# Weight sums of a fast block product: two of four formed by accumulating transfers from GpSimd's queue

## The reference

```python
def swiglu(h, w_gate_up, w_down):
    gu = h @ w_gate_up                     # (512, 1024) @ (1024, 2 * 2816)
    g, u = gu[..., :D_FF], gu[..., D_FF:]
    return (jax.nn.silu(g) * u) @ w_down
```

## Time and profile before

| | |
|---|---|
| median of 3 runs | 1385.08 us (1385.01 to 1385.16) |
| span of the profiled execution, first to last instruction | 1383.4 us |
| own time of the profiled execution beside its span | not listed apart; the runs' median is 1.7 us above the span |
| busy: PE, DVE, ACT, POOL | 1374.1, 961.5, 663.8, 114.9 us |
| granted clock of TensorE, mean of the span | 0.998 of full speed |
| DMA moved | 147.22 MB, mean 106 GB/s |
| transfers issued by GpSimd | none |

### The profile page before, as it was taken

The page is one execution under the profiler, slowest core; times in us unless marked ns, Lnnn a source line. Parts: engine busy times, 40 slices in busy tenths (PEclk is TensorE's granted clock), DMA queues, the critical chain, the costliest instruction groups (busy, mean ns, idle before and its releaser), DMA issues.

```text
span 1383.4 us, 21582 instructions
## 1 busy us (share of the span) xinstructions
PE 1374.1 (99%) x8404; PEld 1225.5 (89%) x8404; DVE 961.5 (70%) x1335; ACT 663.8 (48%) x984; POOL 114.9 (8%) x89
## 2 busy tenths in 40 slices
PE   9999999999999999999999999999999999999997
PEld 8988888889999998998887788988888999998897
DVE  6656556469878877774578755765549888888674
ACT  6633534355455553352756634543454545545341
POOL 0012200110000000110211211100020000000011
PEclk9999999999999999999999999999999999999999
DMA  9721320222323233325321212542132223233321
GB/s 345 268 91 61 107 92 31 91 92 77 122 92 122 93 107 107 120 95 167 97 87 46 82 41 77 185 150 77 46 107 79 105 98 116 93 122 98 116 92 62
DMA packets 42285, 147.22 MB, mean 106 GB/s; under 512 B 5072, under 2 KB 5584, under 8 KB 42192
## 3 DMA queue, kind: packets, MB, share of 16 engines
q1 hardware_dynamic: 38592, 136.79, 28.8%
q10 hardware_dynamic: 3600, 9.12, 1.9%
HBM read 143.80 MB, written 2.10 MB: 105 GB/s over the span
## 4 chain that ended last, share of the span: by engine, by line
PE 96%; DVE 2%; issue 1%; ACT 1%; DMA 0%; POOLq 0%; POOL 0%; ACTq 0%; DVEq 0%
PE acc L2173 17%; PE acc L2175 17%; PE acc L2174 17%; PE acc L2521 8%; PE acc L2522 7%; PE acc L2523 7%; PE acc L2221 3%; PE acc L2223 3%; PE acc L2222 3%; PE aux L2572 2%; PE aux L2571 2%; PE aux L2570 2%; PE aux L2523 1%; PE aux L2522 1%; PE aux L2521 1%
## 5 line engine op out<-in xcount | busy, mean ns | idle before, releaser
L1304 DVE TENSOR_TENSOR w_lo<-raw,w_hi 128x1024 fp32r<-128x1024 f32 x165 | 205.6, 1251 | 123.6 <-ACT w_hi L663 123.2
L663 ACT ACTIVATE w_hi<-raw 128x1024 fp32r<-128x1024 f32 x165 | 173.2, 1052 | 98.6 <-PE acc L2175 55.2
L1229 POOL TENSOR_TENSOR sqsum<-sqsum,tmp 128x512 f32<-128x512 f32 x40 | 60.0, 1501 | 960.3 <-ACT tmp L950 637.0
L2173 PE MATMUL acc<-u_hi,w_hi 128*128 128x512 f32 x352 | 138.7, 394 | 0.0
L2175 PE MATMUL acc<-u_hi,w_lo 128*128 128x512 f32 x352 | 137.2, 390 | 0.0
L2174 PE MATMUL acc<-u_lo,w_hi 128*128 128x512 f32 x352 | 137.1, 389 | 0.0
L2521 PE MATMUL acc<-b_hi,s_hi 128*128 128x256 f32 x432 | 122.4, 283 | 0.0
L2522 PE MATMUL acc<-b_lo,w_hi 128*128 128x256 f32 x432 | 122.3, 283 | 0.0
L2522 PE MATMUL acc<-b_lo,s_hi 128*128 128x256 f32 x432 | 122.2, 283 | 0.0
L2523 PE MATMUL acc<-b_hi,w_lo 128*128 128x256 f32 x432 | 122.2, 283 | 0.0
L2523 PE MATMUL acc<-b_hi,s_lo 128*128 128x256 f32 x432 | 122.2, 283 | 0.0
(11 more groups left out here) (311 smaller groups left out, 3611.0 us busy)
## 6 DMA issues: line engine op xcount, KB each, us to landing
raw<-in_weights SPq DMA_DIRECT2D x253, 512.0 KB, 3.4
hT<-in_x_t ACTq DMA_DIRECT2D x4, 512.0 KB, 8.2
x_tok<-in_x ACTq DMA_DIRECT2D x4, 512.0 KB, 5.1
raw<-in_weights SPq DMA_DIRECT2D x5, 256.0 KB, 6.1
mem_tok<-in_mem ACTq DMA_DIRECT2D x2, 512.0 KB, 5.8
out_h<-out_f SPq DMA_DIRECT2D x2, 512.0 KB, 2.6
memT<-in_mem_t SPq DMA_DIRECT2D x3, 256.0 KB, 6.3
cs_d<-in_cs_d ACTq DMA_DIRECT2D x1, 512.0 KB, 4.3
```

The costliest lines, as they stand in the source:

```text
L663: act.activation(w_hi[:, s, :], raw[:, s, :], ACT.Copy).then_inc(hi_ready, 1)
L1229: pool.tensor_tensor(sqsum[:, :], sqsum[:, :], tmp[:, j % 2, :], ALU.add).then_inc(sq_added, 1)
L1304: dve.tensor_tensor(w_lo[:, s, :], raw[:, s, :], w_hi[:, s, :].bitcast(F32), ALU.subtract)\
L2173: pe.matmul(out, w_h, x_h, start=first, stop=False)
```

## The change

For the pairs q = 2 to 17 of each layer, the first sum (y0 + y1) and the sum that replaces y1 in the ring (x0 + y1) are made by transfers. `weight_sums` on GpSimd's queue, called for q = 2 to 17 behind the layer's last norm: once the plain part's last product is there (`prod_ready`) and, for q of 4 and above, once the low parts of the sums of pair q - 2 are there (`slo_ready`), it issues a transfer of y0 from HBM into the buffer `pre_sum(q)`, which is `sqsum` for even q and `rstd_row` for odd q. Once y has landed in its slot (`raw_in`), it issues a transfer that adds x0 from HBM onto the second half of y in the ring (`third_in`). Once the first transfer has landed (`pre_in`), it issues one that adds y1 from HBM onto `pre_sum(q)`. Each is 128x512 values, 256 KB. ScalarE's `pair_hi` waits for `third_in` in place of `s3_ready`. VectorE's `first_sums` waits for `pre_in` and makes one add, out of `pre_sum(q)` and x0. The high and the low parts of the sums are made by two instructions each, of 512 columns (from `pre_sum`) and of 1024 (from `s_f`). Pairs 0 and 1 of a layer stay as they are, and so do TensorE's instructions and SyncE's loads.

```diff
--- before.py
+++ after.py
@@ -350,6 +350,8 @@
         bhi_ready = sem("bhi_ready")
         blo_ready = sem("blo_ready")
         s3_ready = sem("s3_ready")
+        pre_in = [sem(f"pre_in{e}") for e in range(2)]
+        third_in = [sem(f"third_in{e}") for e in range(2)]
         s_ready = sem("s_ready")
         shi_ready = sem("shi_ready")
         slo_ready = sem("slo_ready")
@@ -478,6 +480,14 @@
 
             n = pair_unit(layer, q) % RING
             return ring[:, n:n + 2, :]
+
+        def pre_sum(q):
+
+            return (sqsum, rstd_row)[q % 2]
+
+        def nth(layer, q):
+
+            return (PAIRS // 2 - 1) * layer + q // 2
 
         def region_a(q):
             return accs[2 * (q % 2)][:, 0:S // 2]
@@ -865,7 +875,10 @@
 
                     n = pair_unit(layer, q)
                     act.wait_ge(raw_in[n % RING], 16 * (n // RING + 1))
-                    act.wait_ge(s3_ready, PAIRS * layer + q + 1)
+                    if q < 2:
+                        act.wait_ge(s3_ready, 2 * layer + q + 1)
+                    else:
+                        act.wait_ge(third_in[q % 2], 16 * nth(layer, q))
                     slot_free(act, n - RING)
                     slot_free(act, n + 1 - RING)
                     act.activation(pair_cols(w_hi, layer, q), pair_cols(raw, layer, q), ACT.Copy).then_inc(hi_ready, 2)
@@ -873,7 +886,10 @@
                 def sum_hi(q):
 
                     act.wait_ge(s_ready, PAIRS * layer + q + 1)
-                    act.activation(s_hi[q % 2][:, :, :], s_f[q % 2][:, :, :], ACT.Copy).then_inc(shi_ready, 1)
+                    if q >= 2:
+                        act.activation(s_hi[q % 2][:, 0, :], pre_sum(q)[:, :], ACT.Copy)
+                    b = slice(1 if q >= 2 else 0, 3)
+                    act.activation(s_hi[q % 2][:, b, :], s_f[q % 2][:, b, :], ACT.Copy).then_inc(shi_ready, 1)
 
                 def copy_product(q, m):
 
@@ -1228,6 +1244,20 @@
                         pool.wait_ge(sq_added, n - 1)
                     pool.tensor_tensor(sqsum[:, :], sqsum[:, :], tmp[:, j % 2, :], ALU.add).then_inc(sq_added, 1)
 
+            def weight_sums(layer, q):
+
+                n, k = pair_unit(layer, q), nth(layer, q)
+                pool.wait_ge(prod_ready, PLAIN * (layer + 1))
+                if q >= 4:
+                    pool.wait_ge(slo_ready, PAIRS * layer + q - 1)
+                pool.dma_start(pre_sum(q)[:, :], d["weights"][n + 1, :, 0:512]).then_inc(pre_in[q % 2], 16)
+                pool.wait_ge(raw_in[(n + 1) % RING], 16 * ((n + 1) // RING + 1))
+                pool.dma_start(raw[:, (n + 1) % RING, 512:1024], d["weights"][n, :, 0:512], accum_op=ALU.add)\
+                    .then_inc(third_in[q % 2], 16)
+                pool.wait_ge(pre_in[q % 2], 32 * k - 16)
+                pool.dma_start(pre_sum(q)[:, :], d["weights"][n + 1, :, 512:1024], accum_op=ALU.add)\
+                    .then_inc(pre_in[q % 2], 16)
+
             pool.wait_ge(var_ready, 1)
             power(rstd_m[:, :], var_m[:, :], MT)
             pool.wait_ge(var_ready, 2)
@@ -1280,6 +1310,8 @@
                 for norm in (3 * layer + 1, 3 * layer + 2):
                     add_squares(norm)
                     norm_power(norm)
+                for q in range(2, PAIRS):
+                    weight_sums(layer, q)
             add_squares(6, KT - 2)
             for e in range(2):
                 pool.wait_ge(aux_free_v, freed_v(aux_at["mean", 6, e]))
@@ -1669,7 +1701,9 @@
                     dve.wait_ge(raw_in[x], 16 * (n // RING + 1))
                     dve.wait_ge(raw_in[y], 16 * (n // RING + 1))
                     if q >= 2:
+                        dve.wait_ge(pre_in[q % 2], 32 * nth(layer, q))
                         dve.wait_ge(product_done, product_at(layer, q - 2, 5))
+                        return step(dve.tensor_tensor(sums[:, 1, :], pre_sum(q)[:, :], raw[:, x, 0:512], ALU.add))
                     i = step(dve.tensor_tensor(sums[:, 0, :], raw[:, y, 0:512], raw[:, y, 512:1024], ALU.add))
                     dve.tensor_tensor(raw[:, y, 512:1024], raw[:, x, 0:512], raw[:, y, 512:1024], ALU.add)\
                         .then_inc(s3_ready, 1)
@@ -1691,7 +1725,11 @@
 
                 def sum_lo(q):
                     dve.wait_ge(shi_ready, PAIRS * layer + q + 1)
-                    dve.tensor_tensor(s_lo[q % 2][:, :, :], s_f[q % 2][:, :, :], s_hi[q % 2][:, :, :].bitcast(F32),
+                    if q >= 2:
+                        dve.tensor_tensor(s_lo[q % 2][:, 0, :], pre_sum(q)[:, :], s_hi[q % 2][:, 0, :].bitcast(F32),
+                                          ALU.subtract)
+                    b = slice(1 if q >= 2 else 0, 3)
+                    dve.tensor_tensor(s_lo[q % 2][:, b, :], s_f[q % 2][:, b, :], s_hi[q % 2][:, b, :].bitcast(F32),
                                       ALU.subtract).then_inc(slo_ready, 1)
 
                 def quarter(q, c):
```

## The result

The changed kernel takes 1392.45 us (median of 4 runs, 1390.67 to 1396.02) against 1385.12 us of the kernel before on the same chip: ratio 1.0056, 95% interval 1.0044 to 1.0069. It is slower by more than the 0.2% that can be told from no change, and above the forecast range, which ended at 1388.5. The profiled execution took 1390.84 us at a span of 1389.1, 5.7 us longer than the span of before.

A forecast was written before the change was run, and what follows sets the result against it. TensorE was taken to bound the kernel, its block-product stages full. Removed from its path 0, added 0 (to 3 us); span 1383.4 us plus 1.7 us carried over gave 1385.1 us, range 1384.0 to 1388.5 us.

The forecast's parts named there:

- A: Rival, slower: GpSimd's transfer issues in the block products held up by VectorE, chain 14.4 us, about 1427 us; chance 0.05.
- B: Rival, slower: accumulating transfers themselves slow, 6.1 us each, chain of 15 to 16.7 us, 1437 to 1464 us; chance 0.03.
- the prediction's own sign: Check in the block products: chain is right if the add's wait for the transfer shows in the first set alone.
- The loop of sets: Set of pair q+2 hangs on the low part of pair q; holds up to a chain of 11.5 us.
- the row taken: Trace row of 512 KB loads, 3.4 us from issue to landing, used as the flight of a 256 KB accumulation.
- D: Rival, faster: matmuls slowed by VectorE's traffic speed up with less of it, perhaps 5 us back, 1380 us; chance 0.02.
- The price list of the tightest place: First set of each layer: late by 3.5 us, costs nothing, 0.5 us left; 2 us longer would cost 1.5 us.
- the term of the chain in that place: First set's plain transfer plus accumulation, issue and flight: 9.8 us, landing at 343.0, still costing nothing.
- the paragraph on what is added: 96 transfers, 25.2 MB more reads; DMA 53% or 67% busy; a pair's loads released by the pair before last's low part.
- C: Rival, a little slower: only first sets late, or GpSimd's queue adds work outside the span; 1388 to 1390 us; chance 0.05.

## Why the prediction was wrong

**What held.** PE was full and gave nothing back for 36 us less of DVE's work. A and B fell: in layer 0's stage DVE waits for a transfer ahead of the first sum in 7 of 16 pairs (8.1 us for sqsum, 5.5 us for rstd_row), yet PE waits only at the first. By the prediction's own sign (the wait of the add shows in the first set alone) the chain was too short for later sets too; their larger room hides it. The loop of sets holds, as booked. POOL's issues take 0.57 to 1.22 us beside DVE's work where 1.5 were taken, so nothing holds them up as A had it. B was nearer than its chance in the price of a flight: the accumulations onto the buffers take 5.4 us in the median, not the 3.4 of the row taken, but its chain of 15 to 16.7 us measured 9.9 in the median. D fell too: starts stay 0.12 us apart. The price list of the tightest place was right in kind: "a chain longer by 2 us would cost 1.5 us a layer, once".

**The step that failed** is the term of the chain in that place: "2 x (1.5 + 3.4) = 9.8 us", with the sentence that "it still costs nothing, with 0.5 us left". The chain measured 11.6 and 10.9 us, and up to 13.1 in the other profiles. The sum of layer 0 by the prediction's own steps, with the measured sizes: the chain is 1.8 us longer; it starts 0.3 us later in the stage (335.43 - 330.08 = 5.35 against 5.04); from the add to L1723 there are 1.76 us instead of 1.2, because L1719 reads what L1706 has just written and waits 0.46 us for it; less the 0.5 us of room. That is 2.2 us, and the gap between the matmul starts is 2.33 - 0.12 = 2.2.

The chain was mis-sized not for the typical set but for its surroundings in the first one. From the issue of the plain transfer to the landing of the accumulation the 32 sets of the trace have a median of 9.9 us, beside the 9.8 booked; that this fits is in part luck, since the halves, 4.9 us each in the sum, are 3.8 and 5.4. The flight was the median of the whole run's loads (3.4 us) and the DMA share that of the stage before the change (30%), while the paragraph on what is added knew that SyncE's loads for a pair are let go by the low part of the pair before last. Nobody asked what lands on the engines at the moment of the first set. It is two loads of 512 KB, which turn the second flight from 4.2 into 8.9 us (the runs with the loads held and not held); and, among them, the ring accumulation ahead of it, without which the flight is 5.7 to 6.4 us. Accumulating holds the engines 2.1 times as long as a plain transfer, and with plain copies throughout the chains are 8.6 and 10.1 us and the loss 0.5. The steady state has 0.5 us more room at the outset and up to 2 us behind it; the first set has 0.5 us altogether.

The Trainium skill (DMA: Bandwidth & Descriptors, Anatomy of one DMA) gives 2.0 us plus the bytes at 436 GB/s, which is 2.6 us for 256 KB. The trace doesn't agree: 3.0 us from issue to landing where plain copies are in use; in the changed kernel 3.8 us for the plain transfers, 3.7 for the ring accumulations, 5.4 for those onto the buffers and 7.9 in the first set. The same page (Queues, rings and completion order) says that an engine takes turns between the queues that have work for it, and drains a whole packet, typically of 9 to 17 descriptors, before it switches. From 342 to 344 q0 and q1 do share the engines (64 and 125 of the profile's packets); from 340 to 342 q0 moved 4 against 130. With the loads held an accumulation's packets are moving 1.2 to 3.2 us after its issue, so here it is the loads that keep them from starting; whether they wait for their turn or are written later stays open.

**What the forecast had as a rival.** C was this case, at 3 to 5 us and a chance of 0.05. Its place was right and its price a little low: it had neither the loads nor the clock, which falls behind some of the waits. A step with 0.5 us of room should have had more: of the span between the bounds of its term, 6.8 to 16.7 us, two thirds lay above the 10.3 us (9.8 + 0.5) from which the first set costs.

**Beyond the mechanism.** The changed kernel's ten runs spread over 6 us (1389.88 to 1396.02); of the 56 runs of before beside the three jobs all but two (1385.41 and 1386.06) lie between 1384.9 and 1385.3. Part is the length of PE's wait, which was 3.2, 4.2 and 4.5 us in three profiles, and part the granted clock: of the first four runs the two long ones, 1394.06 and 1396.02 us, have a mean of 0.996 and 0.994, the short ones, 1390.67 and 1390.84 us, have 0.998 and 0.997. Neither long one was profiled, so where their clock fell isn't known. The up to 1.9 us ahead of the first stage come before any transfer of the change is issued. They are there in some executions of the kernels with transfers and not in others (1.9, 1.1 and 0.1 us in the three profiles of the changed kernel). The runs with one small transfer, 1385.01 to 1385.25, don't have them. What decides it stays open.

No version beats the kernel before, and by the row of PE's starts none of this kind can: the best one equals it.

## What to carry to other kernels

Work taken from an engine that isn't the bound buys nothing, and work put on the DMA in its place must be checked at the first round of each stage, where its trigger is late and its room smallest, not in the steady state. Read there what every queue puts on the engines in those few microseconds, and if the first transfers need nothing of the stage, issue them before it. A chain of two dependent transfers should be priced with the flights of a crowded moment (here 7 to 9 us for the second instead of its median of 5.4). And a short wait of TensorE can cost more than itself, since its clock may fall behind it.

## What the runs showed of the hardware

- An accumulating transfer of 256 KB costs 26.9 us of engine time against 12.9 us for a plain one, by the shares of q0 (9.6% and 5.6%); it goes in 144 packets against 80 (7680 / 96 with plain copies alone; (11776 - 32 x 80) / 64 in the changed kernel).
- GpSimd issues a transfer of 256 KB in 0.57 to 1.22 us while VectorE works 72% of the time.
- The first packets of an accumulation were moving 1.2 to 3.2 us after its issue with SyncE's queue idle, and had not begun in the same stretch with two loads of 512 KB let go some 1 us before it.
- TensorE's clock fell to its lower level for some 3.4 us behind gaps of 3.76, 2.60, 2.38 and 2.02 us between starts in the stages, and stayed at the upper one behind others of up to 3.17 us. Each fall costs some 1.5 us beyond the wait. In the profile of the changed kernel it also fell right at the kernel's start, behind two waits of 1.0 and 0.7 us (the wait list above), and the windows show where most of the 1.9 us came from (start, end, length, then PE's busy time and starts; clock third from the end):

```profile
0.00:8.00 8.00, 5.07 (x25) 4.69 (x26) 1.47 (x3) 3.64 (x7) 0.57 (x8) 1.00 0.69 215
8.00:14.00 6.00, 6.00 (x20) 4.77 (x20) 5.54 (x13) 5.55 (x11) 0.00 (x0) 0.72 1.04 399
```

In the kernel before the same two windows read 1.00 and 1.00, with x27 and x28 starts.
